# The first stage of a three-layer model: order of the first transfers, a row spread by matmul, one table load, 32-row matmuls, and two adds moved

## The chip, the cores and the metric

The kernel runs on one core of a Trainium2 chip, as one program. The metric is the device time of one execution in microseconds, lower is better. Three runs of the kernel before gave the time; a further execution was profiled, and all rows below are from that one.

## The reference

Input is one sequence of 512 tokens by 1024 channels, in float32. Three layers follow each other: a pooling mixer with a swiglu, a latent attention (MLA) with a swiglu, and a differential attention with a mixture of 16 experts. What the change touches is the first mixer:

```python
def rms_norm(x, g):
    xf = x.astype(jnp.float32)
    y = xf * lax.rsqrt(jnp.mean(xf * xf, axis=-1, keepdims=True) + RMS_EPS)
    return (y * g.astype(jnp.float32)).astype(x.dtype)

def pool_mixer(h, w, scale):          # four groups of 256 channels, windows 2, 4, 8, 16
    ...
    for g, win in enumerate(POOL_WINDOWS):
        c = cs[:, :, g]               # running sum over the tokens
        lag = jnp.pad(c[:, :-win], ((0, 0), (win, 0), (0, 0)))
        mean = (c - lag) / jnp.minimum(n_avail, float(win))[:, None]
        outs.append(mean - hf[:, :, g])
    p = jnp.stack(outs, axis=2).astype(h.dtype)
    y = jnp.einsum('bsgc,gcd->bsgd', p, w).reshape(B, S, D)
    return y * scale

h = rms_norm(x, norm_mix[i]);  x = x + pool_mixer(h, pool_w[j], pool_scale[j])
h = rms_norm(x, norm_ffn[i]);  x = x + swiglu(h, ffn_w_gate[i], ffn_w_up[i], ffn_w_down[i])
```

## The kernel before, in words

The 512 tokens are four tiles of 128 (`T = 4`), the channels eight chunks of 128 (`C = 8`). The program is written engine by engine: each engine's instructions stand in one order written by hand, and semaphores join them. Nothing is planned at run time, so an instruction that waits holds back all behind it on its engine.

Weights come in units of 128 x 2048 values (1024 KB) through two buffers (`raw`). Unit 0 is the pool weight, unit 1 the first gate unit of the first swiglu, unit 2 its first up unit. A weight and its operand are each split in a high part (ACT, a copy to a narrower type) and a low part (DVE, the difference), and `product` makes three matmuls out of one: high by low, low by high, high by high (lines 269 to 271).

The first stage runs like this.

- SP issues the transfers in order: four tiles of x, the band table, unit 0, the scale row (one row spread over 128 partitions by the transfer), unit 1, the constants, the swiglu's norm row, unit 2 and so on. ACT's own queue brings the gains.
- ACT touches the gains with a Square and a Sqrt (lines 398 and 400), and then takes for each tile the square with its sum (`square_tile`, L285) and the root (`root_tile`, L293). DVE makes the mean in between (`mean_tile`, L289), then the reciprocal, and scales the tile into `xs` (L441).
- TensorE fills the time with 24 warming matmuls into bank 7. Then it pools: a tile's 128x128 chunk by a band table of 128 columns (L509), and for tiles 1 to 3 also the chunk of the tile before by a table of 16 columns (L511), since up to 15 earlier tokens count. Each of these float32 matmuls is listed as two instructions.
- Tile t's pooled result lies in the banks 2t and 2t + 1. ACT and DVE split it to `AH` and `AL` (`pooled_hi`, `pooled_lo`).
- DVE multiplies unit 0 by the scale row (L451); ACT and DVE split it in eight pieces with the gains (L415, L460).
- TensorE makes the products of tiles 0 to 3. DVE adds each to x (`add`, L472), ACT squares it (L285), DVE applies the norm and row (`gain_tile`, L304), TensorE turns the rows (`turn_tile`, L310), and ACT and DVE split them (`tile_hi` L319, `tile_lo` L323). After eight filling matmuls (`keep_busy`, L278) the swiglu starts, with the first half of the tokens, and needs the low parts of tiles 0 and 1 and of unit 1. Tiles 2 and 3 are turned inside the swiglu's first products.

The order on DVE behind the pooling is: `pooled_lo(3)`, `split_lo` of unit 1, `add(0)`, `gain_tile(0)`, `add(1)`, `gain_tile(1)`, `tile_lo(0)`, `add(2)`, `tile_lo(1)`.

Of the kernel before, what the change touches and what calls it, by code (L numbers as in the profile page):

```python
# [36 lines left out]
P = 128  # L37
# [152 lines left out]
def build_program(nc, stream, experts, x, positions, gains, rows, lams, router, consts, band, out, moe_rows):  # L190
    ctx = ExitStack()
    with ctx:
# [138 lines left out]
        def through_latent_attention(held):  # L331
# [4 lines left out]
            row_here = sem("pool_row_here")  # L336
            ffn_row_here = sem("ffn_row_here")
# [20 lines left out]
            with nc.Block() as block, ExitStack() as tmp:  # L358
# [10 lines left out]
                with ExitStack() as early:  # L369
                    xs = sb("pool_xs", [P, T, D], where=early)  # L370
                    bands = sb("pool_bands", [P, BAND_WIDTH], where=early)
                    scale_row = sb("pool_scale_row", [P, D], where=early)
                    ffn_row = sb("ffn0_row", [P, D], where=early)
                    rows_g = sb("ffn0_rows_g", [P, 2, D], where=early)
                    warm = sb("warm", [P, S], F32R, early)
                memory = hidden_memory("f0", tmp)

                @block.sync
                def _(sp):
                    for t in range(T):  # L380
                        sp.dma_start(X[:, t, :], x[t * P:(t + 1) * P, :]).then_inc(tile_here[t], 16)
                    sp.dma_start(bands[:, :], band[:, :]).then_inc(tables_here, 16)
                    load_unit(sp, 0)
                    sp.dma_start(scale_row[:, :], rows[0:1, :].broadcast_to([P, D])).then_inc(row_here, 16)
                    load_unit(sp, 1)
                    sp.dma_start(cst[:, :], consts[:, :]).then_inc(consts_here, 16)
                    sp.dma_start(ffn_row[:, :], rows[3:4, :].broadcast_to([P, D])).then_inc(ffn_row_here, 16)
                    load_unit(sp, 2)
                    sp.dma_start(final_row[:, :], rows[1:2, :].broadcast_to([P, D])).then_inc(final_row_here, 16)
                    sp.dma_start(pos[:, :], positions[:, :]).then_inc(rope_in, 16)  # L390
                    sp.dma_start(mla_row[:, :], rows[7:8, 0:512].broadcast_to([P, 512])).then_inc(mla_row_here, 16)

                @block.scalar
                def _(act):
                    act.dma_start(gain[:, :], gains[:, :]).then_inc(gains_here, 16)

                    act.wait_ge(gains_here, 16)
                    act.activation(spare[:, 0:1], gain[:, 0:1], ACT.Square).then_inc(copied, 1)
                    act.wait_ge(copied, 1)
                    act.activation(spare[:, 1:2], spare[:, 0:1], ACT.Sqrt).then_inc(copied, 1)  # L400
                    for t in range(T):
                        act.wait_ge(tile_here[t], 16)
                        act.sem_inc(b.added, 1)
                        square_tile(act, b, t, t, xs[:, t, :])
                        root_tile(act, b, t, t)
# [5 lines left out]
                    pooled_hi(0)  # L411
                    act.wait_ge(w_scaled, 1)
# [23 lines left out]
                def _(dve):  # L436
                    dve.memset(warm[:, :].bitcast(F32), 1.0).then_inc(warmed, 1)
                    for t in range(T):
                        mean_tile(dve, b, t, t)
                        invert_tile(dve, b, t, t)  # L440
                        dve.tensor_scalar(xs[:, t, :], X[:, t, :], rstd[:, t:t + 1], None, ALU.mult).then_inc(scaled, 1)  # L441

                    def pooled_lo(t):
# [5 lines left out]
                    dve.wait_ge(row_here, 16)  # L449
                    w4 = raw[:, 0, :].rearrange("p (g k d) -> p g k d", g=4, k=2)  # L450
                    dve.tensor_tensor(w4, w4, scale_row[:, :].rearrange("p (g d) -> p g d", g=4).unsqueeze(2)  # L451
                                      .broadcast_to([P, 4, 2, 256]), ALU.mult).then_inc(w_scaled, 1)
                    pooled_lo(0)
# [11 lines left out]
                    split_lo(dve, 1)  # L465
# [9 lines left out]
                    add(0)  # L475
                    dve.wait_ge(ffn_row_here, 16)
                    gain_tile(dve, f, 0, 0, rows_g, ffn_row)
                    add(1)
                    gain_tile(dve, f, 1, 1, rows_g, ffn_row)
                    tile_lo(dve, f, 0, 0)  # L480
                    add(2)
# [16 lines left out]
                def _(pe):  # L498
                    pe.wait_ge(warmed, 1)
                    for _ in range(24):  # L500
                        pe.matmul(PS[:, 7, :], warm[:, 0:P], warm[:, :], start=True, stop=True)
                    pe.wait_ge(tables_here, 16)
                    for t in range(T):
                        pe.wait_ge(scaled, t + 1)
                        for c in range(C):
# [4 lines left out]
                            if t:  # L510
                                mm = pe.matmul(acc[:, 0:16], xs[:, t - 1, c * P:(c + 1) * P],  # L511
                                               bands[:, 8 * P + 16 * g:8 * P + 16 * (g + 1)], start=False, stop=True)
# [3 lines left out]
                    for t in range(T):  # L516
                        pe.wait_ge(p_lo, t + 1)
                        for g in range(4):
                            for k in range(2):
# [4 lines left out]
                                             WH[:, 0, w], WL[:, 0, w], k == 0, k == 1)  # L524
                        mm.then_inc(mixed if t < T - 1 else unit_used, 1)
                        if t >= 2:
                            turn_tile(pe, f, t - 2, t - 2, rows_g)
                    pe.wait_ge(f.lo, 1)
                    keep_busy(pe, 0, 8, warm)
# [2536 lines left out]
```

## Time and profile before

| | us |
|---|---|
| median of three runs | 1524.1 |
| lowest and highest of them | 1517.73, 1525.69 |
| the profiled execution, time | 1518.95 |
| the profiled execution, span | 1516.9 |
| TensorE busy in the span | 1477.3 |
| first swiglu matmul starts at | 39.77 |

Times in the rows are microseconds from the start of the span unless marked ns. PE is the matmul on TensorE, PEld its weight load, DVE is VectorE, ACT is ScalarE, SPq the queue of SP that issues transfers. A row of the timeline gives start, duration, engine, line, operation, output and input, shapes and the number of instructions that were merged; in square brackets stands how long the engine was idle before, and what released it. A matmul's duration includes its way through the array, so the distance of starts tells the rate. 64*128 in a row is a matmul on 64 rows of the array, 128*128 one on all.

### The profile page before, as it was taken

The numbers are of one execution on the slowest core, as the hardware profiler recorded it, in microseconds if no ns is written. First come the engines' busy times: TensorE is split into PE (matmuls) and PEld (weight loads), VectorE is DVE, ScalarE is ACT, GpSimd is POOL, SyncE is SP. The second block draws the span as 40 slices with busy tenths as digits, with TensorE's granted clock in tenths as the row PEclk, the third lists the DMA queues.
The fourth block names the chain that finished last, engine by engine and source line by source line (L and its number), as shares of the span: only waits on it lengthen the run. The fifth ranks groups of instructions, "written<-read, shape, count | busy, mean of one in ns | idle before, by whom it ended". The sixth has DMA issues, their size and how long they took to land.

```text
span 1516.9 us, 23801 instructions
## 1 busy us (share of the span) xinstructions
PE 1477.3 (97%) x8744; PEld 1279.1 (84%) x8744; DVE 1025.2 (68%) x1275; ACT 796.2 (52%) x1225; POOL 408.7 (27%) x253
## 2 busy tenths in 40 slices
PE   8999999999999999999999999999899999999996
PEld 8999999888887788999998887888567878888875
DVE  6489999442575335899995236335783699998884
ACT  5445555332455424555554224443782478788774
POOL 0567787000000003688770000000130012222211
PEclk9999999999999999999999999999999899999999
DMA  6213323323230122222333232322122499999994
GB/s 251 84 56 110 110 87 110 137 84 125 68 128 1 38 88 84 83 87 106 111 111 118 105 104 77 128 84 84 58 115 108 156 329 385 394 395 394 386 373 114
DMA packets 36217, 226.29 MB, mean 149 GB/s; under 512 B 5272, under 2 KB 5528, under 8 KB 11825
## 3 DMA queue, kind: packets, MB, share of 16 engines
q1 hardware_dynamic: 31392, 212.06, 37.4%
q0 software_dynamic: 4608, 13.22, 3.8%
q8 instruction: 49, 0.80, 0.2%
q14 instruction: 24, 0.19, 0.0%
q10 hardware_dynamic: 144, 0.03, 0.0%
HBM read 215.22 MB, written 13.63 MB: 151 GB/s over the span
## 4 chain that ended last, share of the span: by engine, by line
PE 55%; DVE 4%; DMA 3%; ACT 2%; issue 1%; DVEq 0%; ACTq 0%; SPq 0%; POOLq 0%
PE PS L269 16%; PE PS L271 16%; PE PS L270 16%; DMA eraw<-experts 3%; PE PS L2043 1%; PE PS L2759 1%; PE PS L2054 1%; DVE da_flat L2127 1%; DVE WL L264 1%; PE PS L278 1%; PE PS L2063 1%; PE PS L1834 0%; ACT PS L285 0%; PE PS L2409 0%; ACT WEH L2830 0%
## 5 line engine op out<-in xcount | busy, mean ns | idle before, releaser
L264 DVE TENSOR_TENSOR WL<-raw,WH 128x2048 fp32r<-128x2048 f32 x54 | 127.3, 2358 | 232.4 <-ACT WH L259 232.2
L2893 DVE TENSOR_TENSOR WEL<-eraw,WEH 128x2048 fp32r<-128x2048 f32 x96 | 217.5, 2286 | 20.9 <-ACT WEH L2830 20.6
L259 ACT ACTIVATE WH<-raw 128x2048 fp32r<-128x2048 f32 x52 | 99.5, 1913 | 224.4 <-PE PS L271 224.4
L2830 ACT ACTIVATE WEH<-eraw 128x2048 fp32r<-128x2048 f32 x96 | 182.2, 1914 | 32.6 <-DMA eraw<-experts 22.0
L269 PE MATMUL PS<-AH,WL 128*128 128x256 f32 (+1 forms) x624 | 185.4, 297 | 0.8 <-DVE WL L917 0.3
L271 PE MATMUL PS<-AH,WH 128*128 128x256 f32 (+1 forms) x624 | 183.5, 294 | 0.0
L270 PE MATMUL PS<-AL,WH 128*128 128x256 f32 (+1 forms) x624 | 183.3, 294 | 0.0
L917 DVE TENSOR_TENSOR WL<-plain,WH 128x512 fp32r<-128x512 f32 x136 | 153.2, 1127 | 21.4 <-ACT WH L804 19.6
L269 PE MATMUL PS<-WH,AL 128*128 128x512 f32 (+2 forms) x416 | 154.9, 372 | 5.1 <-DVE AL L323 2.6
L271 PE MATMUL PS<-WH,AH 128*128 128x512 f32 (+2 forms) x416 | 152.8, 367 | 0.0
L270 PE MATMUL PS<-WL,AH 128*128 128x512 f32 (+2 forms) x416 | 152.4, 366 | 0.0
L917 DVE TENSOR_TENSOR WL<-raw,WH 128x512 fp32r<-128x512 f32 x108 | 141.6, 1311 | 0.0
L804 ACT ACTIVATE WH<-plain 128x512 fp32r<-128x512 f32 x136 | 83.9, 628 | 99.2 <-POOL plain L1028 74.0
L269 PEld LDWEIGHTS PS<-AH,WL 128*128 128x128 f32 x624 | 119.1, 191 | 6.1 <-ACT f0part L811 1.7
L271 PEld LDWEIGHTS PS<-AH,WH 128*128 128x128 f32 x624 | 119.0, 191 | 2.5
L270 PEld LDWEIGHTS PS<-AL,WH 128*128 128x128 f32 x624 | 119.0, 191 | 2.5
L1028 POOL TENSOR_TENSOR plain<-raw 128x512 f32<-128x512 f32 x68 | 116.1, 1715 | 17.5 <-PE PS L271 9.1
L269 PE MATMUL PS<-WEH,AH 128*128 128x512 f32 x256 | 101.8, 398 | 1.4 <-DVE AH L2898 1.1
L271 PE MATMUL PS<-WEH,AH 128*128 128x512 f32 x256 | 100.0, 391 | 0.0
L270 PE MATMUL PS<-WEL,AH 128*128 128x512 f32 x256 | 99.7, 390 | 0.0
L1014 POOL TENSOR_TENSOR f1HF<-AH,AL 128x1024 f32<-128x1024 f32 x4 | 9.5, 2398 | 314.2 <-DVE AL L323 314.2
L269 PEld LDWEIGHTS PS<-WH,AL 128*128 128x128 f32 x416 | 78.2, 188 | 18.4 <-issue 2.6
(387 smaller groups left out, 3714.7 us busy)
## 6 DMA issues: line engine op xcount, KB each, us to landing
eraw<-experts SPq DMA_DIRECT2D x96, 1024.0 KB, 15.2
raw<-stream SPq DMA_DIRECT2D x94, 1024.0 KB, 4.9
out<-X SPq DMA_DIRECT2D x5, 512.0 KB, 3.5
moe_rows<-moe_rows_g SPq DMA_DIRECT2D x5, 512.0 KB, 3.0
X<-x SPq DMA_DIRECT2D x4, 512.0 KB, 5.2
ffn_row<-rows SPq DMA_DIRECT2D x2, 512.0 KB, 9.3
final_row<-rows SPq DMA_DIRECT2D x2, 512.0 KB, 6.5
cst<-consts SPq DMA_DIRECT2D x1, 739.5 KB, 13.4
```

Of the source, the lines that this page charges most:

```text
L259: act.activation(WH[:, u % SLOTS, :], raw[:, u % SLOTS, :], ACT.Copy).then_inc(unit_hi, 1)
L264: dve.tensor_tensor(WL[:, u % SLOTS, :], raw[:, u % SLOTS, :], WH[:, u % SLOTS, :].bitcast(F32), ALU.subtract).then_inc(unit_lo, 1)
L269: pe.matmul(acc, lhs_lo, rhs_hi, start=start, stop=False, skip_group_check=resumed)
L270: pe.matmul(acc, lhs_hi, rhs_lo, start=False, stop=False, skip_group_check=resumed)
L271: return pe.matmul(acc, lhs_hi, rhs_hi, start=False, stop=stop, skip_group_check=resumed)
L278: pe.matmul(PS[:, bank, :], some[:, 0:P], some[:, 0:512], start=True, stop=True)
L804: act.activation(quarter(WH, q), source(q, s, odd), ACT.Copy).then_inc(q_hi, 1)
L917: dve.tensor_tensor(quarter(WL, q), source(q, s, odd), quarter(WH, q).bitcast(F32), ALU.subtract).then_inc(q_lo, 1)
L1028: pool.tensor_tensor(sum_at(k, s), x, y, op).then_inc(summed, 1)
L2043: pe.matmul(PS[:, 2 * (i % 2) + m, 0:(q + 1) * P], QT[rows64, h, q * P:(q + 1) * P], KT[rows64, h, 0:(q + 1) * P], start=True, stop=True). ...
L2830: act.activation(WEH[:, k % ESLOTS, :], eraw[:, k % ERAW, :], ACT.Copy).then_inc(unit_hi, 1)
L2893: dve.tensor_tensor(WEL[:, k % ESLOTS, :], eraw[:, k % ERAW, :], WEH[:, k % ESLOTS, :].bitcast(F32), ALU.subtract).then_inc(unit_lo, 1)
```

## The change

- SP's order of transfers: tile 0, bands, tile 1, tile 2, unit 0, tile 3, unit 1. The scale row goes as a single row of 4 KB over ACT's queue, ahead of the gains, and two matmuls with a one-row operand of ones spread it to banks 6 and 7. DVE's multiply of unit 0 reads it there, and tile 3's pooling, which writes those banks, waits for the multiply.
- ACT: one Sqrt on a constant in place of the Square and the Sqrt on the gains. The root takes the mean itself (scale 1/D, bias EPS), and the mean step on DVE is gone.
- DVE: tile 3 is scaled after the multiply of unit 0. Behind the pooling the order is `add(0)`, `split_lo` of unit 1, `add(1)`, `gain_tile(0)`, `gain_tile(1)`, `add(2)`, `tile_lo(0)`, `tile_lo(1)`.
- TensorE: 16 warming matmuls in place of 24. The 16-column matmul takes only the last 32 rows of both operands (the tables are zero above). Tile 0 is turned behind the products of tile 2 as before, tile 1 in the middle of the products of tile 3. Three filling matmuls in place of eight.

```diff
+                    load_tile(0)
                     sp.dma_start(bands[:, :], band[:, :]).then_inc(tables_here, 16)
+                    load_tile(1)
+                    load_tile(2)
                     load_unit(sp, 0)
-                    sp.dma_start(scale_row[:, :], rows[0:1, :].broadcast_to([P, D])).then_inc(row_here, 16)
+                    load_tile(3)
                     load_unit(sp, 1)
...
+                    act.dma_start(scale_row[:, :], rows[0:1, :]).then_inc(row_here, 16)
                     act.dma_start(gain[:, :], gains[:, :]).then_inc(gains_here, 16)
-
-                    act.wait_ge(gains_here, 16)
-                    act.activation(spare[:, 0:1], gain[:, 0:1], ACT.Square).then_inc(copied, 1)
-                    act.wait_ge(copied, 1)
-                    act.activation(spare[:, 1:2], spare[:, 0:1], ACT.Sqrt).then_inc(copied, 1)
+                    act.wait_ge(warmed, 1)
+                    act.activation(spare[:, 0:1], spare[:, 1:2], ACT.Sqrt).then_inc(copied, 1)
                     for t in range(T):
                         act.wait_ge(tile_here[t], 16)
                         act.sem_inc(b.added, 1)
                         square_tile(act, b, t, t, xs[:, t, :])
-                        root_tile(act, b, t, t)
+                        act.wait_ge(b.summed, t + 1)
+                        act.activation(rstd[:, 4 + t:5 + t], rstd[:, t:t + 1], ACT.Sqrt, bias=spare[:, 1:2],
+                                       scale=1.0 / D).then_inc(b.rooted, 1)
...
                     pooled_hi(0)
+                    act.wait_ge(gains_here, 16)
                     act.wait_ge(w_scaled, 1)
...
+                    dve.memset(spare[:, 1:2], EPS).then_inc(warmed, 1)
                     dve.memset(warm[:, :].bitcast(F32), 1.0).then_inc(warmed, 1)
-                    for t in range(T):
-                        mean_tile(dve, b, t, t)
+
+                    def scale_tile(t):
                         invert_tile(dve, b, t, t)
                         dve.tensor_scalar(xs[:, t, :], X[:, t, :], rstd[:, t:t + 1], None, ALU.mult).then_inc(scaled, 1)
+
+                    for t in range(T - 1):
+                        scale_tile(t)
...
-                    dve.wait_ge(row_here, 16)
+                    dve.wait_ge(row_spread, 1)
                     w4 = raw[:, 0, :].rearrange("p (g k d) -> p g k d", g=4, k=2)
-                    dve.tensor_tensor(w4, w4, scale_row[:, :].rearrange("p (g d) -> p g d", g=4).unsqueeze(2)
+                    dve.tensor_tensor(w4, w4, PS[:, 6:8, :].rearrange("p a (g d) -> p (a g) d", g=2).unsqueeze(2)
                                       .broadcast_to([P, 4, 2, 256]), ALU.mult).then_inc(w_scaled, 1)
+                    scale_tile(T - 1)
                     pooled_lo(0)
...
-                    split_lo(dve, 1)
...
                     add(0)
+                    split_lo(dve, 1)
+                    add(1)
                     dve.wait_ge(ffn_row_here, 16)
                     gain_tile(dve, f, 0, 0, rows_g, ffn_row)
-                    add(1)
                     gain_tile(dve, f, 1, 1, rows_g, ffn_row)
+                    add(2)
                     tile_lo(dve, f, 0, 0)
-                    add(2)
                     tile_lo(dve, f, 1, 1)
...
-                    pe.wait_ge(warmed, 1)
-                    for _ in range(24):
+                    pe.wait_ge(warmed, 2)
+                    for _ in range(16):
                         pe.matmul(PS[:, 7, :], warm[:, 0:P], warm[:, :], start=True, stop=True)
+                    pe.wait_ge(row_here, 16)
+                    for side in range(2):
+                        mm = pe.matmul(PS[:, 6 + side, :], warm[0:1, 0:P].bitcast(F32),
+                                       scale_row[:, side * 512:side * 512 + 512], start=True, stop=True)
+                    mm.then_inc(row_spread, 1)
                     pe.wait_ge(tables_here, 16)
                     for t in range(T):
+                        if t == T - 1:
+                            pe.wait_ge(w_scaled, 1)
                         pe.wait_ge(scaled, t + 1)
...
                             if t:
-                                mm = pe.matmul(acc[:, 0:16], xs[:, t - 1, c * P:(c + 1) * P],
-                                               bands[:, 8 * P + 16 * g:8 * P + 16 * (g + 1)], start=False, stop=True)
+                                mm = pe.matmul(acc[:, 0:16], xs[96:P, t - 1, c * P:(c + 1) * P],
+                                               bands[96:P, 8 * P + 16 * g:8 * P + 16 * (g + 1)], start=False, stop=True)
...
+                            if t == T - 1 and g == 1:
+                                turn_tile(pe, f, 1, 1, rows_g)
                         mm.then_inc(mixed if t < T - 1 else unit_used, 1)
-                        if t >= 2:
-                            turn_tile(pe, f, t - 2, t - 2, rows_g)
+                        if t == 2:
+                            turn_tile(pe, f, 0, 0, rows_g)
                     pe.wait_ge(f.lo, 1)
-                    keep_busy(pe, 0, 8, warm)
+                    keep_busy(pe, 0, 3, warm)
```

## Rows read from the trace of the kernel before

**Rows 1.** The page, part 1: TensorE's busy time, share, instructions.

```profile
PE 1477.3 (97%) x8744; PEld 1279.1 (84%) x8744; DVE 1025.2 (68%) x1275; ACT 796.2 (52%) x1225; POOL 408.7 (27%) x253
```

**Rows 2.** Timeline of TensorE, 0 to 45 us; second row from a narrower window.

```profile
1.47 7.04 PE L501 MATMUL PS<-warm 128*128 128x512 f32 x24 [1.47 <-DVE warm L437]
...
6.76 1.52 PE L501 MATMUL PS<-warm 128*128 128x512 f32 x6
...
9.93 2.27 PE L509 MATMUL PS<-pool_bands,pool_xs 128*128 128x128 f32 x18 [1.42 <-DMA pool_bands<-band]
12.04 0.29 PE L511 MATMUL PS<-pool_bands,pool_xs 128*128 128x16 f32 x2
...
22.31 0.29 PE L511 MATMUL PS<-pool_bands,pool_xs 128*128 128x16 f32 x2
22.45 0.36 PE L269 MATMUL PS<-WH,AL 128*128 128x256 f32 x1
...
32.14 1.09 PE L310 MATMUL PS<-cst,ffn_rows_g 128*128 128x128 f32 x8 [0.81 <-DVE ffn_rows_g L304]
...
37.44 2.11 PE L278 MATMUL PS<-warm 128*128 128x512 f32 x8
39.77 0.39 PE L269 MATMUL PS<-AH,WL 128*128 128x256 f32 x1 [0.23 <-DVE AL L323]
```

**Rows 3.** Issues of SP's queue (timeline), then three transfers' KB and us to landing.

```profile
0.75 1.82 SPq L381 DMA_DIRECT2D X<-x  x4
2.62 0.54 SPq L382 DMA_DIRECT2D pool_bands<-band  x1
...
X<-x SPq DMA_DIRECT2D x1, 512.0 KB, 4.0
gain<-gains ACTq DMA_DIRECT2D x1, 27.5 KB, 4.2
...
pool_bands<-band SPq DMA_DIRECT2D x1, 544.0 KB, 7.3
```

**Rows 4.** Timeline of ACT, the first square.

```profile
6.59 1.04 ACT L285 ACTIVATE pool_xs<-X 128x1024 f32<-128x1024 f32 x1
```

**Rows 5.** Timeline of DVE, 8 to 40 us.

```profile
8.38 0.75 DVE L441 TENSOR_SCALAR pool_xs<-X,rstd 128x1024 f32<-128x1024 f32 x1
...
13.93 2.29 DVE L451 TENSOR_TENSOR raw<-raw,pool_scale_row 128x2048 f32<-128x2048 f32 x1 [0.41 <-DMA pool_scale_row<-rows]
...
17.27 3.24 DVE L460 SCALAR_TENSOR_TENSOR WL<-raw,gain,WH 128x256 fp32r<-128x256 f32 x8
...
27.71 1.21 DVE L472 TENSOR_TENSOR X<-X,PS 128x1024 f32<-128x1024 f32 x1
...
30.80 1.28 DVE L304 SCALAR_TENSOR_TENSOR ffn_rows_g<-X,rstd,ffn_row 128x1024 f32<-128x1024 f32 x1
...
38.49 1.23 DVE L323 TENSOR_TENSOR AL<-PS,AH 128x1024 fp32r<-128x1024 f32 x1
```

**Rows 6.** Timeline of TensorE in the latent attention, 464 to 468 us.

```profile
464.63 0.49 PE L1471 MATMUL PS<-KR,QR 64*128 64x128 f32 x4
465.05 0.71 PE L1475 MATMUL PS<-KN,QN 128*128 128x128 f32 x4
465.69 0.70 PE L1471 MATMUL PS<-KR,QR 64*128 64x256 f32 x4
466.32 1.13 PE L1475 MATMUL PS<-KN,QN 128*128 128x256 f32 x4
467.39 0.92 PE L1471 MATMUL PS<-KR,QR 64*128 64x384 f32 x4
```

**Rows 7.** Timeline of TensorE near 1200 us, then a window (PEclk: granted clock).

```profile
1196.89 3.65 PE L2409 MATMUL PS<-router_weights,moe_turned 128*128 128x20 f32 x32
...
1204.00:1206.00 2.00, 2.00 (x5) 0.99 (x3) 1.84 (x10) 0.00 (x0) 0.00 (x0) 0.50 0.08 31
```

**Rows 8.** Windows: length, busy us by engine (PE first), granted clock, DMA share.

```profile
40.00:50.00 10.00, 10.00 (x86) 10.00 (x86) 7.36 (x7) 4.30 (x6) 0.00 (x0) 1.00 0.31 107
```

More of the change, by code:

```diff
@@ L336, in through_latent_attention @@
             row_here = sem("pool_row_here")
+            row_spread = sem("pool_row_spread")
             ffn_row_here = sem("ffn_row_here")
@@ L371, in through_latent_attention @@
                     bands = sb("pool_bands", [P, BAND_WIDTH], where=early)
-                    scale_row = sb("pool_scale_row", [P, D], where=early)
+                    scale_row = sb("pool_scale_row", [1, D], where=early)
                     ffn_row = sb("ffn0_row", [P, D], where=early)
@@ L379, in _, with load_tile @@
                 def _(sp):
-                    for t in range(T):
+                    def load_tile(t):
                         sp.dma_start(X[:, t, :], x[t * P:(t + 1) * P, :]).then_inc(tile_here[t], 16)
+                    load_tile(0)
                     sp.dma_start(bands[:, :], band[:, :]).then_inc(tables_here, 16)
+                    load_tile(1)
+                    load_tile(2)
                     load_unit(sp, 0)
-                    sp.dma_start(scale_row[:, :], rows[0:1, :].broadcast_to([P, D])).then_inc(row_here, 16)
+                    load_tile(3)
                     load_unit(sp, 1)
@@ L436, in _ @@
                 def _(dve):
+                    dve.memset(spare[:, 1:2], EPS).then_inc(warmed, 1)
                     dve.memset(warm[:, :].bitcast(F32), 1.0).then_inc(warmed, 1)
-                    for t in range(T):
-                        mean_tile(dve, b, t, t)
+                    def scale_tile(t):
                         invert_tile(dve, b, t, t)
                         dve.tensor_scalar(xs[:, t, :], X[:, t, :], rstd[:, t:t + 1], None, ALU.mult).then_inc(scaled, 1)
+                    for t in range(T - 1):
+                        scale_tile(t)
                     def pooled_lo(t):
```

## The prediction

> **What bounds the kernel now.** The page first: TensorE is busy for 1477.3 of 1516.9 us [rows 1]. So what counts is when TensorE can go on, and the first stage is read on its own timeline [rows 2]. It has four parts. Twenty-four warming matmuls from 1.47 to 8.51. A wait of 1.42 us for the band table, then the pooling matmuls from 9.93. The split products of the pool weights from 22.45. Two turnings (L310), eight filling matmuls (L278), and the first swiglu matmul at 39.77. Between 9.93 and 39.77 TensorE waits little, 0.81 us ahead of the first turning and 0.23 at the end. From 39.77 on it works without a break (ten us of ten in the next window [rows 8], and in the three behind it), and the diff touches nothing behind it, so I count the change as the shift of that 39.77 and carry it to the end undiminished.
>
> **The transfers.** The first tile is issued at 0.75 and lands 4.0 us later, at 4.75; the bands are issued at 2.62 and land 7.3 later, at 9.92 [rows 3]. Between the two landings come three tiles and the bands, 3 x 512 + 544 = 2080 KB in 5.17 us, 402 KB per us. In the new order, from 4.75 on: bands 6.1, tile 1 7.4, tile 2 8.65, unit 0 11.2, tile 3 12.5, unit 1 15.0, constants 16.9, swiglu row 18.2. The last two landed later before, as a whole 512 KB broadcast falls out of the queue. The scale row (4 KB) now goes first on ACT's queue and the gains behind it; the gains took 4.2 us to land [rows 3], so I put the row at about 5 and the gains at about 5.5, and both are wanted later than that.
>
> **ACT and DVE ahead of the pooling.** ACT waited for the gains (0.74 + 4.2 = 4.94 [rows 3]), loaded a second table behind them and started tile 0 at 6.59 only [rows 4], 1.84 after it had landed. Now nothing but two issues and one table load stands ahead of the tile, all of it before 4.75, and the first square starts at 4.85. From the start of a square to the scaled tile it took 8.38 + 0.75 - 6.59 = 2.54 us [rows 4, 5]; the mean step on DVE falls out and the root takes an operand more, so about 2.4. Tiles 0, 1, 2 are scaled at about 7.3, 9.9 and 11.3. DVE's multiply of unit 0 took 2.29 us and now reads PSUM; a subtract that reads 1024 elements of PSUM took 1.23 [rows 5], against 1.15 for half of the 2.29, so at most 2.5. It runs from 11.3 to 13.8, and tile 3 is scaled behind it at 15.0.
>
> **The start of the pooling on TensorE.** Eight warming matmuls fewer: late in the row six took 1.52 us [rows 2], and less the tail of the last that is 0.23 each. The sixteen end at 8.51 - 8 x 0.23 = 6.7. Then the two spreading matmuls, each two instructions of 512 columns. In the attention rows 128 columns more of one instruction cost 0.107 (below), so 4 x 0.43 = 1.7, and a change of form 0.2: they end at 8.6, and pooling starts at 8.7, by TensorE's own work, as bands (6.1) and tile 0 (7.3) are there. That is 1.2 us earlier than 9.93.
>
> **The 32-row matmuls.** This is the large term. Before, the 24 pairs of a 128-column and a 16-column product (two instructions each, 128 rows) came every (22.31 - 12.04) / 23 = 0.4465 us, four instructions of 0.111 [rows 2]. The 16 columns themselves cost next to nothing; each instruction costs its weight load. The load of a 32-row form isn't in the trace, but a switch between forms is. The latent attention alternates four 64-row instructions with four of 128 rows [rows 6]. At 128 columns the starts are 0.42 and 0.64 apart, at 256 columns 0.63 and 1.07. The 64-row ones run two abreast (0.21 per 128 columns for the four), the 128-row ones one by one (0.43 for the four). So each group pays 0.42 - 0.21 = 0.21 and 0.64 - 0.43 = 0.21 us beyond its columns, whatever the width: work of the other form has to leave before the first load, and that load is then bare. The change makes 48 such groups out of the 24 pairs, and a 32-row group has no neighbour to run abreast with, as all of them sit on rows 96 to 127.
>
> The cost of a pair: the 128-row group 0.21 + 2 x 0.107 = 0.42. In the 32-row group the second load follows the first: bare load and leaving 0.21, a load 0.11, the columns 0.02, together 0.34. Sum 0.76 against 0.4465. The high bound takes two full loads beside the 0.21 in the small group, 0.865 for the pair. A low one lets the second load hide, as the four 64-row loads do behind each other: 0.65. I take 0.76, since both instructions load the same rows and nothing shown lets them overlap. Before, pooling took 22.45 - 9.93 = 12.52 us, so 24 x 0.4465 and 1.8 for tile 0. After: 8.7 + 1.8 + 24 x 0.76 = 28.7 (26.1 to 31.3), against 22.45.
>
> By the Trainium skill, TensorEngine Tiling (Array Packing), section Key Properties, changing the tiling mode drains the engine; the 0.21 us of the attention rows agrees with it. By TensorE: Matmul & The Clock Gate, section LDWEIGHTS, a 32x128 load takes as long as a 128x128 one; if only that rule held, without the drain, a pair would stay at its 0.4465, and no row here shows a 32-row load.
>
> **What is hidden.** TensorE's new wait for the scaled weights, ahead of tile 3, ends at 13.8; tile 3 is reached at 22.7, or at 17.6 if a pair stays at 0.4465. Only DVE's multiply stands before it, and tile 3's scaling behind that (15.0) is in time too. ACT's first eviction starts behind the last root at 14.0, its eight weight pieces end near 18.3 and DVE's low parts, some 1 us behind them, at 19.5 (DVE's eight took 3.24 us [rows 5]; I give ACT's the same). With pairs at 0.4465 pooling ends at 21.2, so this has 1.7 us of cover even there. The constants (16.9) are wanted then and are hidden.
>
> **From the end of pooling, E, to the swiglu.** Before 39.77 - 22.45 = 17.3. After, on TensorE: three tiles of products end at E + 8.65 (24 x 0.12 each). On DVE: the last pooled subtract to E + 2.6, add 0 when tile 0 is mixed, E + 3.0 to 4.2, the low split (2.29) to 6.5, add 1 (1.21) to 7.7, reciprocal and gain (0.2 + 1.28) to 9.2 [rows 5]. The split now stands ahead of the second add instead of the first, but it still delays gain 0 by 2.3 together with add 1's 1.2: TensorE waits 0.55 for gain 0. Turning 0 to 10.1 (1.09 less overlap), two groups of tile 3 to 11.6, turning 1 to 12.6 (gain 1 is there at 10.7), the other two groups to 14.0, three filling matmuls to 14.7. Beside it ACT's second eviction 12.7 to 13.7 and DVE's low part (1.23) to 14.9, which ends last. So 14.95 instead of 17.3, a gain of 2.4: the second turning lies inside tile 3, and five filling matmuls are gone. Bounds: TensorE's bare work here, 14.1, and 17.3 if the gain is late. The later swiglu waits (third gain, unit 2) keep at least the distance they had.
>
> **Sum.** Swiglu starts at 28.7 + 14.95 = 43.7 against 39.77: + 3.9 us, made of - 1.2 (start), + 7.5 (24 pairs at + 0.314) and - 2.4. The bounds of a pair give + 1.3 to + 6.5. The profiled execution had a span of 1516.9 and a time of 1518.95, which become 1520.8 and 1522.9. The three runs shown have their median at 1524.1, 5 above that execution; on it the same 3.9 gives 1528.0.
>
> **Rivals.** *Switching costs nothing* (the 32-row form takes its turn like the 16-column one before): E is 8.7 + 12.5 = 21.2, swiglu at 36.15, - 3.6 us, 1520.5. For it speaks that no 32-row row is in the trace; against it that the 0.21 holds at several widths and both ways. This is the case on the other side: it decides from a pair at 0.60 us downwards, where the 1.2 and 2.4 are not yet eaten (3.6 / 24 = 0.15 per pair). *The small loads are hidden too*: pooling would be shorter than 10 us, but DVE's low weights (19.5) hold the products back: swiglu at 34.5, - 5.3, 1518.8. *The clock falls*: behind 32 matmuls of 20 columns in 3.65 us the granted clock is 0.50 in the stretch from 1204 to 1206, though TensorE is at work in it [rows 7]; that is 1.2 instead of 2.4 GHz. The pooling with 128 streamed columns in every 0.38 us is thinner than now, but far denser than that. If it fell at 15 us, 18 pairs would cost 0.76 more each, and the first products some 1.5, what the warming lost at its start (7.04 against 24 x 0.23 [rows 2]): + 3.9 + 13.7 + 1.5, 1543.2.
>
> **How the numbers follow.** Forecast 0.66 (1525.4 to 1530.6 on the median), switching for nothing 0.20, small loads hidden 0.04, clock 0.10. A half per cent, 7.6 us, is about what a measurement of this kernel can tell from no change. The forecast and the two gaining rivals all lie within it. Slower than that is the clock case and the forecast's upper end with the spread of the runs (1517.73 to 1525.69): 0.10 + 0.07. Faster takes a gaining rival and that spread: 0.06. Same 0.77. The range goes from the rival at 1520.5 less 4 of spread, 1516, to the forecast's upper bound 1530.6 and 5 above, 1536, and leaves the clock case out.
>
> **What would show it.** The bands' wait gone and pooling begun at 8.7. The 16-column matmuls listed with 32 rows, and their starts 0.76 apart instead of 0.45. Pooling ending near 28.7. From there 15 us to the first swiglu matmul, at 43.7. The granted clock at 1.00 in all of it. Wrong would be: pairs under 0.60, a clock under 1.00 between 12 and 40 us, or the scaled weights (13.8) late enough to be waited for. A different shift at the end of the kernel than at the swiglu would mean that later stages don't follow the first one.

## The result and the profile after

The changed kernel takes 1538.59 us (median of four, 1537.46 to 1541.11) against 1523.17 for the kernel before (four runs). The ratio on record is 1.0117, 95% interval 1.0096 to 1.0139; the quotient of these two medians is 1.0101, inside it. So it is slower by 1.0 to 1.2%; 1528.0 had been forecast, with a range up to 1536. The profiled execution has a span of 1535.7, 18.8 more than before.

The page of the changed kernel, parts 1 and 2 (the last two lines are the granted clock in 40 slices of 38 us, of the changed kernel and then, for comparison, of the kernel before):

```profile
PE 1498.4 (98%) x8735; PEld 1294.7 (84%) x8735; DVE 1024.0 (67%) x1272; ACT 795.6 (52%) x1223; POOL 409.1 (27%) x253
...
PEclk6999999999999999999999999999999889999998
...
PEclk9999999999999999999999999999999899999999
```

TensorE is busier than before by 21 us with nine instructions fewer, and the clock's first digit is a 6 where it was a 9. The timeline of TensorE, to be laid beside [rows 2]:

```profile
1.51 5.31 PE L512 MATMUL PS<-warm 128*128 128x512 f32 x16 [1.51 <-DVE warm L444]
6.75 1.98 PE L515 MATMUL PS<-pool_scale_row,warm 1*128 1x512 f32 x4
8.66 2.27 PE L527 MATMUL PS<-pool_bands,pool_xs 128*128 128x128 f32 x18
10.87 0.39 PE L529 MATMUL PS<-pool_bands,pool_xs 32*128 32x16 f32 x2
11.19 0.49 PE L527 MATMUL PS<-pool_bands,pool_xs 128*128 128x128 f32 x2
11.60 0.39 PE L529 MATMUL PS<-pool_bands,pool_xs 32*128 32x16 f32 x2
...
14.56 0.40 PE L529 MATMUL PS<-pool_bands,pool_xs 32*128 32x16 f32 x2
14.89 0.80 PE L527 MATMUL PS<-pool_bands,pool_xs 128*128 128x128 f32 x2
15.62 0.60 PE L529 MATMUL PS<-pool_bands,pool_xs 32*128 32x16 f32 x2
16.15 0.80 PE L527 MATMUL PS<-pool_bands,pool_xs 128*128 128x128 f32 x2
...
37.04 0.60 PE L529 MATMUL PS<-pool_bands,pool_xs 32*128 32x16 f32 x2
37.57 0.58 PE L269 MATMUL PS<-WH,AL 128*128 128x256 f32 x1
...
54.51 0.39 PE L269 MATMUL PS<-AH,WL 128*128 128x256 f32 x1 [0.24 <-DVE AL L323]
```

Pooling starts at 8.66, and the first pairs (a 32-row and a 128-row group) are 11.60 - 10.87 = 0.73 us apart. From 14.89 on the same pair takes 1.26 (16.15 - 14.89), with no wait anywhere. Pooling ends at 37.57 and the swiglu starts at 54.51, 14.7 us late. The windows of the changed kernel say why (length, busy us of PE, PEld, DVE, ACT, POOL, then the granted clock, DMA share, GB/s):

```profile
5.00:10.00 5.00, 5.00 (x25) 3.17 (x24) 1.84 (x4) 3.70 (x8) 0.00 (x0) 1.00 1.04 428
10.00:15.00 5.00, 5.00 (x32) 4.10 (x30) 4.01 (x6) 2.74 (x7) 0.00 (x0) 0.98 1.01 419
15.00:20.00 5.00, 5.00 (x17) 3.96 (x17) 5.00 (x11) 4.04 (x9) 0.00 (x0) 0.50 0.42 169
...
35.00:40.00 5.00, 5.00 (x20) 4.44 (x21) 1.23 (x1) 2.32 (x2) 0.00 (x0) 0.50 0.00 0
40.00:45.00 5.00, 5.00 (x36) 5.00 (x35) 2.27 (x2) 1.45 (x2) 0.00 (x0) 0.79 0.00 0
```

The granted clock goes from 1.00 (2.4 GHz) to 0.50 (1.2 GHz) at 14.8, and comes back at 42, when the products have run for 4.4 us. PE stands at 5.00 of 5.00 all the time: the busy share doesn't show that the engine gets through its work more slowly.

The other 4.1 us of the span lie behind the first stage. The latent attention starts at 481.2 against 464.6, a shift of 16.6; the differential attention at 1087.4 against 1070.2, 17.2; the experts' first turning at 1251.2 against 1231.9, 19.3; the span ends 18.8 later. The first step is one wait on TensorE at the exit of the first swiglu's loop, released by nothing but its own issue, which the kernel before doesn't have (timeline of the changed kernel):

```profile
285.97 0.50 PE L269 MATMUL PS<-WH,f0FL 128*128 128x512 f32 x1 [1.73 <-issue]
```

The small step in the middle, 0.6 us, goes with a fall of the clock near 946 that the kernel before doesn't have: the six traces with a fall between 926 and 950 take 606.2 to 606.5 us from the latent to the differential attention, the other eight 605.2 to 605.6. The last step is the clock at the router. In the trace of the changed kernel it averages 0.57 over 20 us (first window), in that of the kernel before 0.53 over 11 us (second window):

```profile
1218.00:1238.00 20.00, 18.85 (x65) 14.86 (x65) 13.82 (x48) 11.21 (x11) 3.13 (x3) 0.57 0.49 178
```

```profile
1202.00:1213.00 11.00, 10.32 (x33) 8.06 (x34) 7.52 (x42) 4.28 (x8) 2.11 (x2) 0.53 0.38 128
```

### The profile page after: what moved, and what is told of

It reads as the page before. It is cut to its first block, busy times and chain, and to the rows that moved or that the text cites. A ratio compares the mean times of both kernels' runs of the same rounds, so it can differ in the third digit from the quotient of the medians.

```text
span 1535.7 us, 23780 instructions
## 1 busy us (share of the span) xinstructions
PE 1498.4 (98%) x8735; PEld 1294.7 (84%) x8735; DVE 1024.0 (67%) x1272; ACT 795.6 (52%) x1223; POOL 409.1 (27%) x253
## 4 chain that ended last, share of the span: by engine, by line
PE 55%; DVE 4%; DMA 3%; ACT 1%; issue 1%; DVEq 0%; ACTq 0%; SPq 0%; POOLq 0%
PE PS L269 16%; PE PS L271 16%; PE PS L270 16%; DMA eraw<-experts 3%; PE PS L2063 1%; PE PS L2779 1%; PE PS L278 1%; PE PS L2074 1%; DVE da_flat L2147 1%; PE PS L2083 1%; PE PS L1854 0%; PE PS L2429 0%; DVE WL L264 0%; ACT WEH L2850 0%; DVE da_flat L2161 0%
## 5 line engine op out<-in xcount | busy, mean ns | idle before, releaser
L1048 POOL TENSOR_TENSOR plain<-raw 128x512 f32<-128x512 f32 x68 | 116.4, 1720 | 16.6 <-PE PS L271 8.7
L269 PEld LDWEIGHTS PS<-WH,AL 128*128 128x128 f32 x416 | 79.6, 191 | 18.8 <-issue 2.6
## 6 DMA issues: line engine op xcount, KB each, us to landing
eraw<-experts SPq DMA_DIRECT2D x96, 1024.0 KB, 15.4
```

What stands on the lines that cost most here:

```text
L269: pe.matmul(acc, lhs_lo, rhs_hi, start=start, stop=False, skip_group_check=resumed)
L1048: pool.tensor_tensor(sum_at(k, s), x, y, op).then_inc(summed, 1)
```

## The experiments

Each is a small edit of the kernel before or after. "Pooling" and "swiglu" are the starts on TensorE's timeline, "products" is the end of the pooling. The ratios are to the kernel before, measured along with them (medians 1520.68 for e1 to e6, e8 and e9, 1519.98 for the others). e4 and e6 have two runs each, e2 and e10 four, the others ten to twelve; each has one trace.

| kernel | pooling | products | swiglu | clock 10 to 40 us | ratio (95%) |
|---|---|---|---|---|---|
| before | 9.93 | 22.45 | 39.77 | 1.00 | 1 |
| changed | 8.66 | 37.57 | 54.51 | 0.50 from 14.8 | 1.0117 (1.0096 to 1.0139) |
| e1 all rows | 9.73 | 23.88 | 38.83 | 0.50 for 3.4 us, then 1.00 | 0.9998 (0.9983 to 1.0012) |
| e2 only 32 rows | 9.91 | 37.33 | 55.29 | 0.50 from 18.2 | 1.0109 (1.0087 to 1.0132) |
| e3 grouped | 9.71 | 24.72 | 39.68 | as e1 | 1.0005 (0.9992 to 1.0018) |
| e4 64 rows | 8.97 | 37.70 | 54.85 | 0.50 from 15.4 | 1.0117 (1.0092 to 1.0141) |
| e5 padded | 11.18 | 23.70 | 38.64 | 1.00 | 1.0004 (0.9987 to 1.0020) |
| e6 thin, all rows | 9.80 | 41.63 | 59.78 | 0.50 from 16.1 | 1.0129 (1.0110 to 1.0147) |
| e7 tail only | 9.70 | 22.23 | 37.15 | 1.00 | 0.9986 (0.9977 to 0.9995) |
| e8 row by transfer | 7.52 | 20.89 | 35.91 | 1.00 | 0.9993 (0.9984 to 1.0001) |
| e9 spread on all rows | 9.30 | 21.72 | 36.66 | 1.00 | 0.9996 (0.9985 to 1.0007) |
| e10 dense | 9.84 | 33.76 | 48.71 | as e1 | 1.0061 (1.0046 to 1.0077) |
| e11 transfer, code moved | 8.42 | 20.84 | 35.85 | 1.00 | 0.9982 (0.9973 to 0.9992) |
| e12 all rows, code moved | 9.72 | 22.25 | 37.19 | 1.00 | 0.9992 (0.9983 to 1.0001) |

**e1: the 32 rows taken back.**

```diff
-                                mm = pe.matmul(acc[:, 0:16], xs[96:P, t - 1, c * P:(c + 1) * P],
-                                               bands[96:P, 8 * P + 16 * g:8 * P + 16 * (g + 1)], start=False, stop=True)
+                                mm = pe.matmul(acc[:, 0:16], xs[:, t - 1, c * P:(c + 1) * P],
+                                               bands[:, 8 * P + 16 * g:8 * P + 16 * (g + 1)], start=False, stop=True)
```

> The changed kernel with the 16-column matmul back on all 128 rows; all its other edits stay. Theory A (the switches between the 32-row and the 128-row form are the cause of everything lost, the clock's fall included): pairs at 0.45 us, granted clock 1.00 up to 60 us, pooling from 8.7 to 21.2, swiglu starts at 36.2 against 39.77 of before, time ratio to before 0.9976. Theory B (the clock falls because there are eight warming matmuls fewer and two one-row matmuls behind them): the clock falls near 15 us here too, pairs at 0.89 from there, swiglu near 44, ratio 1.003.

The ratio is 0.9998, so this one edit held all of the loss. But neither theory is quite met. Timeline and one window of e1:

```profile
9.73 3.78 PE L527 MATMUL PS<-pool_bands,pool_xs 128*128 128x128 f32 x18
...
13.91 0.29 PE L529 MATMUL PS<-pool_bands,pool_xs 128*128 128x16 f32 x2
```

```profile
10.00:15.00 5.00, 5.00 (x33) 5.00 (x32) 4.22 (x6) 2.76 (x6) 0.00 (x0) 0.66 1.02 425
```

The clock was at 0.50 from 10.2 to 13.6 and then came back, and pairs are at 0.445 from there on. So it can fall early in the pooling too, without any 32-row matmul, but then it comes back after 3.4 us and stays. That and a warming that took 1 us longer put the swiglu at 38.83 in place of 36.2.

**e2: the same edit alone, on the kernel before.** The diff is that of e1, the other way round.

> The kernel before with one edit of the change, the 16-column matmul on the last 32 rows. Theory A: pairs at 0.735 us, the clock falls about 4 us after the first pair (12 us), then 1.26 a pair, pooling ends near 39 and swiglu starts near 58, ratio 1.012. Theory B: the 24 warming matmuls hold the clock at 1.00, pooling ends near 29.4, swiglu at 46.7, ratio 1.0045.

The ratio, 1.0109, is theory A's to 0.1%. The landmarks are a little earlier than its 39 and 58 (37.33 and 55.29), since the clock fell only at 18.2, 6.1 us behind the first 32-row matmul, where the changed kernel's fell after 3.9. The eight more warming matmuls don't explain that: e6 below has the same 24, and its clock falls 4.2 us behind its first pair. Timeline of e2:

```profile
17.61 0.49 PE L509 MATMUL PS<-pool_bands,pool_xs 128*128 128x128 f32 x2
18.03 0.47 PE L511 MATMUL PS<-pool_bands,pool_xs 32*128 32x16 f32 x2
18.43 0.80 PE L509 MATMUL PS<-pool_bands,pool_xs 128*128 128x128 f32 x2
19.15 0.60 PE L511 MATMUL PS<-pool_bands,pool_xs 32*128 32x16 f32 x2
19.68 0.80 PE L509 MATMUL PS<-pool_bands,pool_xs 128*128 128x128 f32 x2
```

**e3: six groups in place of 48.** In this order the 16-column terms are not added up as in the reference; the kernel stands for its time alone.

```diff
-                            if t:
+                        if t:
+                            for c in range(C):
...
                                 mm = pe.matmul(acc[:, 0:16], xs[96:P, t - 1, c * P:(c + 1) * P],
```

> The changed kernel with a tile's eight 128-column matmuls first and its eight 32-row ones behind them, 6 groups in place of 48. Theory A with a 32-row load at the full 0.107 us: a tile takes 16 x 0.107 + 0.21 twice, 3.85 us, swiglu starts near 37.1, clock 1.00 throughout, ratio 0.998. Rival, 32-row loads are cheaper than that: a tile takes 2.6 to 3.2 us and swiglu starts at 35 to 36. Rival, the thin stretch of eight small matmuls is enough for the clock to fall: swiglu at 42 or later.

Timeline of e3:

```profile
15.11 1.95 PE L533 MATMUL PS<-pool_bands,pool_xs 32*128 32x16 f32 x16
16.99 2.05 PE L527 MATMUL PS<-pool_bands,pool_xs 128*128 128x128 f32 x16
18.97 1.95 PE L533 MATMUL PS<-pool_bands,pool_xs 32*128 32x16 f32 x16
```

Sixteen 32-row instructions take 1.88 us (16.99 - 15.11), sixteen 128-row ones 1.98. In the changed kernel two of them take 0.32 (11.19 - 10.87) and 0.41 (11.60 - 11.19). So 14 more cost 1.56 and 1.57, 0.11 each in either form, and what a group pays once is 0.10 and 0.19. The 32-row matmul is no cheaper, and the price, 0.29 for the two groups of a pair, is for the change of form. By the Trainium skill (TensorE: Matmul & The Clock Gate, LDWEIGHTS) a load's time goes by its columns, not its rows; the 0.11 in both forms agrees. A tile takes 3.86 us as forecast. The clock didn't hold throughout: it fell as in e1, from 10.2 to 13.6, and with that and the slower warming the swiglu starts at 39.68 in place of 37.1. Once back, it stays at 1.00, for all the stretches of eight small matmuls.

**e4: 64 rows in place of 32** (`xs[64:P, ...]`, `bands[64:P, ...]`).

> The changed kernel with the last 64 rows in place of the last 32. If the switch is paid for any change of form, pairs cost 0.735 us at 2.4 GHz as with 32 rows. If the clock falls because few columns pass per us, it falls near 15 us here too and swiglu starts near 54.5, ratio 1.01. If it falls because few rows are in use, it holds longer or throughout, swiglu near 43, ratio 1.002.

The same pair (0.74), the same fall at about 15.4, the same time. Whether the slice has 32 or 64 rows doesn't matter.

**e6: thin, but one form.** Two more 16-column matmuls on all rows behind each pair of tiles 1 and 2.

```diff
                                 mm = pe.matmul(acc[:, 0:16], xs[:, t - 1, c * P:(c + 1) * P], ...)
+                                if t < T - 1:
+                                    for _ in range(2):
+                                        pe.matmul(PS[:, 7, 0:16], xs[:, t - 1, c * P:(c + 1) * P], ...)
```

> The kernel before with two more 16-column matmuls on all 128 rows behind each pair of tiles 1 and 2 (into bank 7, read by nobody): no change of form, but a pair takes 0.89 us for the same 128 wide columns, so it is thinner in columns than the pair with 32 rows (0.735). If few columns per us make the clock fall, it falls within 4 to 6 us of 12 us, and swiglu starts at 54 or later. If changing the form, or using few rows, is needed for it, the clock holds at 1.00 and swiglu starts at 39.8 + 16 x 0.445 = 46.9.

Timeline of e6; L515 are the added ones:

```profile
14.29 0.47 PE L509 MATMUL PS<-pool_bands,pool_xs 128*128 128x128 f32 x2
14.59 0.29 PE L511 MATMUL PS<-pool_bands,pool_xs 128*128 128x16 f32 x2
14.73 0.60 PE L515 MATMUL PS<-pool_bands,pool_xs 128*128 128x16 f32 x4
15.18 0.47 PE L509 MATMUL PS<-pool_bands,pool_xs 128*128 128x128 f32 x2
...
17.73 0.77 PE L509 MATMUL PS<-pool_bands,pool_xs 128*128 128x128 f32 x2
...
19.44 0.78 PE L509 MATMUL PS<-pool_bands,pool_xs 128*128 128x128 f32 x2
```

At 14.29 a step is 0.89 us, at 17.73 it is 1.71. The clock fell with no change of form, all 128 rows in use and not one idle moment. Nor is it the number of matmuls: eight in 0.89 us are as many per us as the kernel before's four in 0.4465, where the clock holds. So theory A was right about the edit and wrong about its mechanism: the switch isn't needed for the fall, and what the falling kernels share is that the 128-column matmuls come further apart.

**e10: the changed kernel, made dense.** All 48 changes of form stay; 12 filling matmuls of 512 columns are added (and two waits moved ahead, so that their banks are free; TensorE doesn't idle in them).

```diff
+                            if t and c % 2 == 0:
+                                keep_busy(pe, (None, 4, 7, 0)[t], 1, warm)
                             if t:
                                 mm = pe.matmul(acc[:, 0:16], xs[96:P, t - 1, c * P:(c + 1) * P],
```

> The changed kernel, 32-row matmuls and all, with one filling matmul of 512 columns behind every second 128-column one of tiles 1 to 3 (12 in all, into banks that are free; two waits are moved ahead for that). If the clock falls because few columns pass per us, it holds here: pairs at 0.735 plus 0.12, pooling ends near 31, swiglu near 46, ratio 1.004, faster than the changed kernel by 8 us although it does more work. If changing the form is enough for the fall, the clock falls near 15 us, swiglu starts at 57 or later, ratio 1.013.

Timeline and a window of e10:

```profile
15.16 0.48 PE L278 MATMUL PS<-warm 128*128 128x512 f32 x1
15.57 0.39 PE L533 MATMUL PS<-pool_bands,pool_xs 32*128 32x16 f32 x2
15.89 0.49 PE L529 MATMUL PS<-pool_bands,pool_xs 128*128 128x128 f32 x2
...
17.29 0.39 PE L533 MATMUL PS<-pool_bands,pool_xs 32*128 32x16 f32 x2
```

```profile
20.00:25.00 5.00, 5.00 (x28) 3.73 (x28) 1.23 (x1) 1.02 (x1) 0.00 (x0) 1.00 0.92 342
```

Two pairs and a filling matmul take 17.29 - 15.57 = 1.72 us up to the end of the pooling, at clock 1.00. A warming slower by 1.2 us and the same short fall as in e1 lie ahead of it, and make the 2.7 us between 46 and 48.71. It does strictly more work than the changed kernel and reaches the swiglu 5.8 us earlier: the 11.5 us that the fall costs (worked out below) are saved, and 2.9 for the fillings, 1.6 for the early fall and 1.2 for the warming are paid. Its ratio is lower by 0.0056, 8.5 us, but of that some 1.7 us are the wait at the loop's exit, which e10's trace hasn't (see e12). The 8.9 us that its swiglu is later than the kernel before's are the switches' 6.9 (worked out below), the fillings' 2.9 (12 x 0.24), and the early fall's 1.6, less the gains at the start and behind the pooling.

**e5, e9: the one-row matmuls.** e5 is e1 with 24 warming and four filling matmuls. e9 is e1 with the row's buffer, now of 128 rows, cleared by DVE first, and the spreading matmuls on all rows; the row's transfer is issued only behind the clearing, and TensorE waits 0.45 us for it.

```diff
 # e5
-                    for _ in range(16):
+                    for _ in range(24):
...
-                    keep_busy(pe, 0, 3, warm)
+                    keep_busy(pe, 0, 4, warm)
 # e9
+                    dve.memset(scale_row[:, :], 0.0).then_inc(warmed, 1)
...
-                        mm = pe.matmul(PS[:, 6 + side, :], warm[0:1, 0:P].bitcast(F32),
+                        mm = pe.matmul(PS[:, 6 + side, :], warm[:, 0:P].bitcast(F32),
```

> The all-row kernel (changed kernel, 16-column matmul on 128 rows) with 24 warming matmuls again and four filling ones, which brings TensorE's instruction count back to that of before. Theory F (the 1.5 to 1.7 us that TensorE waits on its own queue at the exit of the first swiglu's loop depends on where the code lies): the wait is gone, or changed, and the latent attention follows the swiglu's start by 424.8 us as before instead of 426.4. Rival: the wait belongs to the changed transfers and stays. The clock: if eight more warming matmuls hold it, it stays at 1.00 and swiglu starts at 38 to 39; if the one-row matmuls alone make it fall, it falls within 4 us behind them here too. Ratio 0.998 to 1.000.

> The all-row kernel with the row spread by matmuls on all 128 rows: the operand's other 127 rows are cleared by DVE first, so the same 512 columns pass with the same result. If few rows in use make the clock fall, it stays at 1.00 and pairs are at 0.45 throughout. If the waits around the spreading make it fall, it falls near 10 us here too. Swiglu at 37 to 38.5, ratio 0.998 to 1.000.

The clock holds in both. e5's attention follows its swiglu by 424.5 us, as before, and e9's by 426.6: the wait at the loop's exit is gone in the one and there in the other. But it also holds in e12, which has e1's one-row matmuls as they are and at the same moment (7.81 against 7.82). So a fall doesn't follow from them alone, and with one trace of each kernel the runs don't settle what decides it. One thing goes along with it: in e1, e3 and e10, where the clock fell early, the sixteen warming matmuls had taken 6.4 to 6.5 us, in the changed kernel, e4 and e12, where it didn't, 5.3 to 5.7. The warming starts at half the rate of its end in every trace, though the clock reads 1.00 there, and of the kernels with one-row matmuls those three kept that rate longest. No run here tests whether that is the cause. What is certain is its price, 1.6 us: the products start at 23.88 in e1 and at 22.25 in e12, with pooling begun at 9.7 in both. Timelines of e1 and of e12, up to the one-row matmuls:

```profile
1.50 6.39 PE L512 MATMUL PS<-warm 128*128 128x512 f32 x16 [1.50 <-DVE warm L444]
7.82 1.98 PE L515 MATMUL PS<-pool_scale_row,warm 1*128 1x512 f32 x4
```

```profile
2.19 5.70 PE L515 MATMUL PS<-warm 128*128 128x512 f32 x16 [2.19 <-DVE warm L445]
7.81 1.98 PE L518 MATMUL PS<-pool_scale_row,warm 1*128 1x512 f32 x4
```

**e7: only the edits behind the pooling, on the kernel before.**

```diff
-                    split_lo(dve, 1)
...
                     add(0)
+                    split_lo(dve, 1)
+                    add(1)
...
+                            if t == T - 1 and g == 1:
+                                turn_tile(pe, f, 1, 1, rows_g)
...
-                    keep_busy(pe, 0, 8, warm)
+                    keep_busy(pe, 0, 3, warm)
```

> The kernel before with only the edits behind the pooling: the two adds and the low split in the new order, the second turning inside tile 3, three filling matmuls. By the prediction's step from the end of pooling to the swiglu: 14.95 us in place of 17.3, swiglu at 37.4, clock 1.00. If the gain is late the stretch stays at 16 us or more. The wait at the first loop's exit may appear, as five filling matmuls fewer move the code. Ratio 0.998 to 1.000.

Two rows of e7's timeline:

```profile
22.23 0.36 PE L269 MATMUL PS<-WH,AL 128*128 128x256 f32 x1
...
37.15 0.39 PE L269 MATMUL PS<-AH,WL 128*128 128x256 f32 x1 [0.24 <-DVE AL L323]
```

14.92 us, where 14.95 had been worked out. These edits alone make the kernel faster, 0.9986 with an interval below 1. The wait at the loop's exit doesn't appear.

**e8: the row by transfer again.** e1 without the spreading matmuls and tile 3's wait for the weights, and with the broadcast transfer right behind unit 0.

```diff
                     load_unit(sp, 0)
+                    sp.dma_start(scale_row[:, :], rows[0:1, :].broadcast_to([P, D])).then_inc(row_here, 16)
                     load_tile(3)
...
-                    for side in range(2):
-                        mm = pe.matmul(PS[:, 6 + side, :], warm[0:1, 0:P].bitcast(F32), ...)
```

> The all-row kernel with the scale row spread by the transfer again (512 KB, behind unit 0), without the one-row matmuls and without tile 3's wait for the weights. Theory G (the one-row matmuls cost their 1.9 us and, through the clock, 1.8 more): pooling starts at 7.4, clock at 1.00, products at 20 to 21, swiglu at 35 to 36, 4 us ahead of before, ratio 0.9975 to 0.9985. Rival: the later transfers (tile 3 at 13.8, row 12.5) hold the pooling of tile 3 or the weights back, swiglu at 37.5 or later, ratio 1.000.

Swiglu at 35.91, as theory G has it; at the end 1.1 us of the span are lost in place of 3.9 gained (1518.0). The attention starts 425.4 behind the swiglu (before 424.8), and by the landmarks most of the rest, 4.3 us, went between 1066 and 1233, where the clock fell at 1137 and for 20 us at 1198. That is one execution; the twelve runs give a ratio of 0.9993.

**e11, e12: the code moved.** Ahead of the warming, instructions that only count up a semaphore nobody waits for: 13 in e8's kernel, nine in e1's.

```diff
+                    for _ in range(9):
+                        pe.sem_inc(moved, 1)
                     pe.wait_ge(warmed, 2)
```

> The kernel with all rows and the row by transfer, and ahead of the warming 13 instructions on TensorE's queue that only count up a semaphore nobody waits for; they lie in the 1.5 us in which TensorE waits anyway. Swiglu near 35.9 as without them. If the wait at the loop's exit depends on where the code lies, the 0.5 us at 266 us goes and the latent attention starts 424.8 us behind the swiglu in place of 425.4. What is left of the 3.9 us at the end then depends on the clock's falls at 1100 and 1200 us; ratio 0.9975 to 0.9995.

> The all-row kernel with nine such counting instructions ahead of the warming and nothing else. If the 1.5 us at the exit of the first swiglu's loop depend on where the code lies, they are gone and the attention follows the swiglu by 424.8 us; if they belong to the other edits, 426.4 stays. The clock: the one-row matmuls are in it, so it may fall for some 3.5 us between 9 and 15 as in the all-row kernel, or hold, depending on when they come. Ratio 0.998 to 1.000.

e1 had the wait at the loop's exit (timeline), and e12 hasn't: its attention starts at 461.9, 424.7 behind the swiglu, where e1's starts 426.4 behind.

```profile
269.98 0.50 PE L269 MATMUL PS<-WH,f0FL 128*128 128x512 f32 x1 [1.46 <-issue]
```

The wait of 1.4 to 1.7 us stands in the traces of the changed kernel, e1, e3, e4 and e9, and in none of before, e2, e5, e6, e7, e10, e11 and e12 (e8 has 0.5 us). Nine harmless instructions move it away: it goes with how many instructions lie ahead, and not with what the edits do. That the place of the code is the reason is the likely reading. The counting instructions also hold the warming back, from 1.50 to 2.19 in e12 and to 2.79 in e11, where they had been meant to lie in a wait. But the time alone doesn't explain it: e12's swiglu starts at 37.19, between e9's 36.66 and e1's 38.83, which both have the wait. e11 is the fastest of all, 1517.12 against 1519.98, ratio 0.9982, and its interval leaves out 1.

## Why the prediction was wrong, step by step

**The start of the pooling** was right: 8.66 for 8.7, 1.27 us earlier. The bands landed at 1.21 + 4.9 = 6.1 as worked out, and nothing waited for a transfer.

**The 32-row pair** was right at 2.4 GHz: 0.735 for 0.76, inside 0.65 to 0.865. The way there holds too: two groups that each pay for the change of form, and a load as dear as before (0.41 for the 128-row group, 0.32 for the other, for 0.42 and 0.34). By the Trainium skill (TensorEngine Tiling (Array Packing), Key Properties) changing the tiling mode drains the engine; the 0.10 and 0.19 us that a group pays once agree with that. The price of the 48 changes alone is 24 x (0.735 - 0.4465) = 6.9 us.

**What is hidden** was right. DVE's multiply ran from 11.26 for 2.28 us, and tile 3 was scaled at 15.0, long before TensorE came to it.

**From the pooling's end to the swiglu** was right as a term (14.92 in e7), and 16.9 in the changed kernel only because the first 4.4 us of products ran at half clock.

**The step that failed is the clock.** The sum took the granted clock to be 1.00 all through and its fall at nothing; the fall stood only among the rivals, with a chance of 0.10 and 15.2 us, and 15 us as the moment. That rival is what happened, at 14.8. The ground for the low chance was that 128 columns in every 0.38 us are "far denser" than the router's narrow matmuls, the only fall that the prediction drew on. That compares with one end only: the rows showed a stream in which the clock is down and one, the old pooling, in which it holds, and the new pairs lay between them. The changed kernel, e2 and e4 show that the clock falls with pairs at 0.735, e6 that it falls with steps of 0.89 and no change of form, and e10 that it stays up when filling matmuls stand between the same pairs. The price: 18 pairs at 1.26 - 0.735 = 0.525 more each are 9.5 us (the rival had 0.76 each, since it doubled the switch's price too), and 2.0 for the products. 43.7 + 9.5 + 2.0 - 24 x 0.025 = 54.6, and 54.51 was measured.

**That the shift of the swiglu goes to the end undiminished** was nearly right for the first stage's sake, but two things behind it move by themselves: the wait at the loop's exit, 1.4 to 1.7 us, and the clock's falls further on. From the start of the differential attention to the experts' first turning, where the falls near 1100 and 1200 us lie, the fourteen traces take 161.7 (before, e2, e3, e5 and e9) to 167.8 us (e7), the changed kernel 163.7. Together they make the 4.1 us beyond the 14.7, and they hid what e1 and e8 gain at the swiglu, 0.9 and 3.9 us.

What stays open: why the clock fell early in e1, e3 and e10 and not in e5 and e12, why it fell 6.1 us behind the first pair in e2 and 3.9 to 4.2 in the changed kernel, e4 and e6, and what sets the length of the late falls. The first and the last cost about as much as the gains that are left.

## What to carry to other kernels

A narrow matmul on a slice of the rows wasn't cheaper here than one on all of them (0.11 us either way), and between full ones the two changes of form cost 0.29 us together; if such matmuls are worth having, put all of one form together. When an edit stretches TensorE's matmuls apart without making it idle, price it at both clocks: the busy share says 100% at either, and only the granted clock, or the distance of starts, tells. And an effect of 2 us at the front of a kernel is judged by its landmark in the trace, since a wait that comes and goes with the instruction count and the clock further on move the total by as much.

## What the runs showed that was not expected

The clock falls under a TensorE that never idles (e6: steps of 0.89 us, 128 rows, no gap), and filling matmuls bring a kernel with more work to its swiglu 5.8 us earlier (e10). The Trainium skill (TensorE: Matmul & The Clock Gate, Why this matters for your kernels) warns of idle gaps between bursts; in e6 no gap was needed. In the changed kernel the clock came back 27 us later, after 4.4 us of products at half speed. And with nine instructions more that only count (e12), a wait of 1.5 us at 270 us is gone.
